# First mixer of a two-block network: the turns of finished heads held back to the end of the V gemm

## The reference, cut to what matters

```python
def even_mixer(x, w_in, w_out, ...):
    h = x @ w_in                                   # 512x1024 @ 1024x3584
    qa, ka, va, hq, hf, hi, hg = jnp.split(h, cuts, axis=-1)
    o_a = diff_attention(qa, ka, va, ...)          # 4 heads, two softmaxes each, output 512x512
    o_b = hgrn2(hq, hf, hi, hg, ...)               # 4 heads of a gated recurrence, output 512x512
    return jnp.concatenate([o_a, o_b], axis=-1) @ w_out
```

## Time and profile before

| | |
|---|---|
| median of 3 runs | 2228.19 us (2227.71 to 2228.74) |
| the profiled execution's own time | 2232.27 us |
| its span on the core | 2230.4 us |
| granted TensorE clock over the span | 0.981 |
| TensorE matmul busy | 2142.6 us, 96% of the span |
| VectorE busy | 1311.1 us, 59% |
| ScalarE busy | 1038.1 us, 47% |
| DMA | 335.83 MB, 151 GB/s on average |

### The profile page before, as it was taken

How to read it: one execution, slowest core, us unless ns; L and a number is a source line. 1 busy time by engine, 2 the same in 40 slices (tenths; PEclk the granted TensorE clock), 3 DMA queues, 4 the chain that set the end, 5 groups by cost and what they waited for, 6 DMA issues and landing times.

```text
span 2230.4 us, 28802 instructions
## 1 busy us (share of the span) xinstructions
PE 2142.6 (96%) x10977; PEld 1778.6 (80%) x10977; DVE 1311.1 (59%) x2250; ACT 1038.1 (47%) x1643; POOL 152.1 (7%) x247
## 2 busy tenths in 40 slices
PE   8998989999999999988999999999999999999997
PEld 7886768888888877768888888878788888888885
DVE  4564766344346357776443445647735566987696
ACT  4443645233234356554332333533743353887685
POOL 0000011000002000002000002102000001111111
PEclk9999989999999999999999999999999998999999
DMA  6235425323233254433333232443335336999995
GB/s 202 81 128 175 134 84 189 95 76 113 86 102 96 81 180 137 135 98 118 119 94 95 87 111 82 143 133 130 101 120 177 104 103 243 333 367 328 289 360 194
DMA packets 210065, 335.83 MB, mean 151 GB/s; under 512 B 15856, under 2 KB 103168, under 8 KB 209920
## 3 DMA queue, kind: packets, MB, share of 16 engines
q1 hardware_dynamic: 204880, 320.80, 43.3%
q0 software_dynamic: 5040, 13.11, 2.7%
HBM read 298.21 MB, written 40.89 MB: 152 GB/s over the span
## 4 chain that ended last, share of the span: by engine, by line
PE 82%; DVE 7%; DMA 4%; ACT 3%; POOL 2%; issue 2%; SPq 0%; DVEq 0%; POOLq 0%; ACTq 0%
PE ps L180 76%; PE ps L183 6%; POOL SM L215 2%; DVE WL L195 1%; ACT ST L191 1%; DMA ONDP<-qkd 1%; POOL SM L212 1%; DMA qkd<-ST 1%; DVE X L205 1%; ACT WH L191 1%; DVE BR L195 0%; DVE JP L195 0%; DMA XG<-hd,IDX 0%; DMA KTr<-ktd 0%; DVE X L195 0%
## 5 line engine op out<-in xcount | busy, mean ns | idle before, releaser
L195 DVE TENSOR_TENSOR WL<-RAW,WH 128x1024 fp32r<-128x1024 f32 x455 | 548.4, 1221 | 263.3 <-ACT WH L191 257.2
L191 ACT ACTIVATE WH<-RAW 128x1024 fp32r<-128x1024 f32 x455 | 475.5, 1057 | 416.5 <-PE ps L180 335.5
L180 PE MATMUL ps<-XH,WH 128*128 128x512 f32 (+1 forms) x880 | 324.0, 368 | 2.9 <-DVE WL L195 2.9
L180 PE MATMUL ps<-XL,WH 128*128 128x512 f32 (+1 forms) x880 | 321.5, 365 | 0.0
L180 PE MATMUL ps<-XH,WL 128*128 128x512 f32 (+1 forms) x880 | 321.3, 365 | 0.0
L180 PE MATMUL ps<-WH,XH 128*128 128x512 f32 (+1 forms) x736 | 295.1, 401 | 4.7 <-DVE XL L195 2.8
L180 PE MATMUL ps<-WH,XL 128*128 128x512 f32 (+1 forms) x736 | 285.9, 388 | 0.0
L180 PE MATMUL ps<-WL,XH 128*128 128x512 f32 (+1 forms) x736 | 285.8, 388 | 0.0
L180 PE MATMUL ps<-WH,HH 128*128 128x512 f32 x512 | 200.0, 391 | 0.0
L180 PE MATMUL ps<-WH,HL 128*128 128x512 f32 x512 | 199.3, 389 | 0.0
L180 PE MATMUL ps<-WL,HH 128*128 128x512 f32 x512 | 199.2, 389 | 0.0
(11 more groups left out here) (339 smaller groups left out, 3126.8 us busy)
## 6 DMA issues: line engine op xcount, KB each, us to landing
RAW<-in_ffn_w_dram SPq DMA_DIRECT2D x128, 512.0 KB, 3.9
RAW<-in_w_gate_dram SPq DMA_DIRECT2D x60, 512.0 KB, 8.0
RAW<-in_w_down_dram SPq DMA_DIRECT2D x60, 512.0 KB, 10.8
RAW<-in_w_up_dram SPq DMA_DIRECT2D x57, 512.0 KB, 10.1
RAW<-in_w_in_dram SPq DMA_DIRECT2D x30, 512.0 KB, 4.5
qkd<-ST SPq DMA_DIRECT2D x24, 512.0 KB, 2.8
RAW<-in_ev_w_in_dram SPq DMA_DIRECT2D x20, 512.0 KB, 4.8
RAW<-in_ple_w_gate_dram SPq DMA_DIRECT2D x16, 512.0 KB, 3.7
```

The source lines that it names most:

```text
L180: return self.go(ns).matmul(o, lhsT=l, rhs=x, start=st, stop=sp)
L191: return self.go(0.83 * n + 55.0 + (130.0 if bias is not None else 0.0) + (100.0 if acc is not None else 0.0)).activation(o, i, f, scale=s ...
L195: return self.go(1.04 * n + 68.0).tensor_tensor(o, a, b, op)
```

## The change

In `turns_on` the wait ahead of each finished head's transposes, and the need that the planner is given for it, gets a third term: the last product of the va gemm. Nothing else is edited.

```diff
         def turns_on():
             for kt in (4, 5, 6, 7, 0, 1, 2, 3):
-                pe.wait_ge(*(yield [("fin", kt), TP.ask(("onT", kt))]))
+                pe.wait_ge(*(yield [("fin", kt), ("u", "va", 0, 3), TP.ask(("onT", kt))]))
                 b = pe.slot("onT", kt)
                 for T in range(4):
                     t = pe.tr(b[:, cols(T)], ON[:, T, cols(kt)], ident[:, :])
```

## The result

The changed kernel took 2196.8 us, median of 4 executions (2195.4 to 2199.6), against 2228.3 before (4 executions): ratio 0.986, 95% interval 0.9843 to 0.9877. That is 31.5 us less. The forecast was 17 us less and a range that ended at 2199; the direction was right, the size was not. The profiled execution took 2196.51 us, its span is 2194.7. The profiled execution of the kernel before, at 2232.27 us, lay 4.0 us above its median, so two profiles set side by side show 35.8 us where the medians show 31.5.

What follows compares the result with a forecast made beforehand. TensorE, busy 96% of the span, was the bound, so only its idle time and slow clock could be won. 12.0 - 4.0 - 2.1 + 11.1 = 17.0 us saved, giving a median of 2211 us, range 2199 to 2222.

Steps and rivals of the forecast that it cites:

- 12.0 for the head: Between 190 and 210 us: the fourth recurrence head goes early, removing idle time and slow clock; 12.0 us saved.
- 13.1 for the tail: At attention's end before wod: idle time and slow clock of the last head alone; 13.1 us, of which 11.1 counted won.
- 2.1 for more mixing: Where attention and filler mix: 32 us more of mixing adds idle time by plan-chip mismatch; cost 2.1 us, bounds 0 and 4.
- 2.0 at the tail: At attention's end before wod: a remainder of 2.0 us kept as not won.
- the 5.1 of the middle: From 210 to 290 us: TensorE's 5.1 us of idle time, which the forecast left in.
- 4.0 us for turns behind va: Behind va: moved turns 0.9, wait 2.3, other slices and slow clock 0.8; cost 4.0 us, bounds 0.9 and 6.
- everything fills: Rival: attention also covers the start of woh and the two ple waits; 29 us saved, 2199 us; chance 0.10.
- V as the limit: In attention: a head's last output product needs V's last quarter, after va's last product and a DRAM trip; until about 210 us.
- 3.0 + 3.3 = 6.3 us: Slow-clock losses priced in the two gains: around 190 to 210 us and at attention's end; 6.3 us.
- attention still ends last: Rival: at attention's end, only some 1 of 11.1 us is won; 6.9 us saved, 2221 us; chance 0.12.
- slower, by the weights: Rival: on SyncE's queue, attention loads make some 16 weight tiles late; 23 us slower, 2251 us; chance 0.04.
- No change: Rival: the fourth head's keys still run after va, only two turns move; 2228 to 2229 us; chance 0.04.

Runs made afterwards that it cites:

- one_parked: Changed kernel, but head 4 keeps the old rule: turned early, its bank held to the end of va; 2196.8 us, ratio 0.9862.
- hold_attention: Changed kernel, but all loads and evictions of attention also wait for va's last product; 2216.4 us, ratio 0.9942.
- keys_first: Changed kernel, but heads 4 and 5 may be turned before va ends, behind the fourth head's keys; 2206.1 us, ratio 0.9904.
- hold_to_qk1: Changed kernel, but loads and evictions of attention also wait for qk1's last product; 2207.6 us, ratio 0.9900.

## Why the prediction was wrong in size

**What bounds the kernel, and the mechanism:** right. Both banks were held, the fourth head and all of attention stood behind them: one_parked shows that both banks have to be held for the loss, hold_attention parts the head from attention, keys_first shows that attention needs a bank too. The keys went at 145.06 (forecast 146), the loads at 163.1 (forecast 159; 158.4 to 163.1 in four profiles), va ended at 209.7 (forecast 203).

**The gross gain:** 12.0 for the head and 13.1 for the tail. hold_attention, which keeps the first and loses the second, is 15.7 us shorter in the mixer and 10.9 overall; the step from it to the changed kernel is 11.7 to 15.8 in the mixer. Both terms stood.

**The step that failed is the idle time that I left in.** From 145 us to the first norm there were 24.5 us of it; the forecast took 18.8 away and put 2.3 behind va, 2.1 for more mixing and 2.0 at the tail back, and left the 5.1 of the middle: some 12 us. 5.5 remained (4.9 to 6.7 in four profiles). Term by term: of the 4.0 us for turns behind va, 0.5 of idle time and the 0.9 of moved turns were paid. V products of attention lie between the pairs, but that is the smaller part of it, since hold_attention without them idled only 1.3: four heads are turned and evicted in overlap, and my 2.3 was the chain of a head that is turned alone. Of the 2.0 at the tail none was paid. Of the 5.1 + 2.1 for mixing, 2.8 were paid up to 190, mostly one wait of 2.28 behind a late weight tile, 0.9 up to 210, and 1.7 in the middle. The idle time makes 6.6 of the 10.4 us by which the mixer gained more than the forecast's 17.0; the other 3.8 are busy time.

I had listed nearly this outcome as a rival, "everything fills", at 0.10, with 29 us; the mixer gave 27.4. Its reason, that attention's work covers the waits of the filler, fits the rows: the waits for ST and XL in the middle are gone. It was not tried apart from the rest.

**V as the limit** stood: the first head was finished 7.9 to 9.2 us behind the last reload of V in eight profiles in which attention had its loads and a bank early. Attention ended at 279.6 (275.5 to 279.9 in four profiles), at or past the late end of the 260 to 275 forecast. What was wrong is the slack. The forecast saw some 20 us between attention's end and wod, since it kept 13 us of waits and turns in that stretch; the filler ended at 283 and not at 293, so the last head was only some 3 us early. Nor did that slack make attention's start free: 11.5 us later (hold_to_qk1) cost 5 to 9 us in the mixer.

**The clock:** I priced the slow products at 3.0 + 3.3 = 6.3 us, gave back 0.8, and 0.9 of moved turns come in: 4.6 us less busy time. It fell by 8.4 in the first two profiles and by 7.6 between the means of all. I had priced only the products close to the two holes; the stretch between them, too, went from a clock of 0.96 to 1.00. The estimate by the Trainium skill, "TensorE: Matmul & The Clock Gate", section "HAM oscillation" (slow time by one half), was 8.0 for the two windows alone. Over the whole stretch the same estimate gives 0.08 x 174.7 - 0.02 x 147.3 = 11.0 against the 8.4, so this trace does not decide for it; it also counts the slow clock of the time in which TensorE stood idle.

**The range** took the rest of the program as fixed. It ended at 2199 and the measurement fell 2.2 below. 8.3 us of the profiled difference came from behind the mixer, 3.3 between the means of all profiles; the second measurement of the changed kernel, at 2199.3, would have been just inside. That part of the miss is luck, the mixer's 27 against 17 is not. A sum over one profiled execution should have had a few us on either side for it.

**The rivals:** "attention still ends last" did not happen, nor did "slower, by the weights": in the changed kernel one weight tile came late, once, and cost 2.28 us and a spell of slow clock (the same wait was 2.02, 2.29 and 0.87 us in its other profiles). "No change" is out, and with it the reading that more free banks bring nothing; one_parked adds that it is the first free bank, not the second, that brings it.

What stays open: what makes the part behind the mixer short in one execution and long in another; the runs show only that it happens with the same instructions in the same order.

## What to carry to other kernels

When a buffer is filled long before anyone may empty it, count the buffers of its ring and look at who else asks that ring: one held buffer of two was free of charge, the second stopped everything behind it. When two streams of work cover each other's waits, do not carry the idle time of the old overlap into the new one: I left 12 us, and 5.5 remained. Then look for the balance: the kernel in which attention ended some 14 us earlier was 12 us slower, the one in which it ended last 17 to 20. And take the size of what can be told from many executions, not from four that happen to agree.

## What the runs showed of the hardware that I had not expected

Four executions of the kernel before lay within 1.0 us of each other (2227.7 to 2228.7), and 19 executions of it in another series over 13.1 us (2222.6 to 2235.7), with the mean granted clock from 0.979 to 0.985. A single wait of 2.28 us was followed by products at half rate (0.43 us apart) in the first profile of the changed kernel, and the window 145 to 165 had a granted clock of 0.83; in the second profile the same wait was 0.87 us and that window's clock 1.00. That is most of the 4.1 us between their first norms. In two further profiles the wait was 2.02 and 2.29 us, that window's clock 0.91 and the first norm at 292.6 and 291.1.
